# One part of x is loaded by ScalarE's queue instead of SyncE's in a decoder-layer kernel

## What is computed

```python
h = rmsnorm(x, norm_mix_g[l])
proj = jnp.einsum('bsd,de->bse', h, w_in[l])
dq, dk, dv, mq, mk, mv, gate = jnp.split(proj, SPLITS, axis=-1)
...
y = jnp.concatenate([d_out, m_out], axis=-1) * jax.nn.silu(gate)
x = x + jnp.einsum('bse,ed->bsd', y, w_out[l])
h2 = rmsnorm(x, norm_mem_g[l])
mn = rmsnorm(mem, mem_norm_g[l])
q = jnp.einsum('bsd,de->bse', h2, w_q_mem[l]).reshape(B, S, MEM_HEADS, HEAD_DIM)
kv = jnp.einsum('bmd,de->bme', mn, w_kv_mem[l])
...
return rmsnorm(x, final_g)
```

## Time and profile before

| | us |
|---|---|
| median of 3 runs | 571.14 (571.1 to 571.47) |
| the profiled execution, whole run | 571.27 |
| its span, from the first to the last instruction | 569.5 |
| TensorE busy | 560.7 (98% of the span) |
| VectorE busy | 428.2 (75%) |
| ScalarE busy | 408.7 (72%) |
| bytes moved | 123.58 MB, 217 GB/s on the mean |

### The profile page before, as it was taken

One profiled execution on the slowest core, in us unless ns is written; L12 is line 12 of the kernel. 1 busy time (PEld: TensorE's weight loads), 2 busy tenths in 40 slices (PEclk: granted clock), 3 DMA queues, 4 the chain that ended last, 5 costly groups with the idle time before them and its releaser, 6 DMA issues.

```text
span 569.5 us, 8631 instructions
## 1 busy us (share of the span) xinstructions
PE 560.7 (98%) x2648; PEld 467.8 (82%) x2648; DVE 428.2 (75%) x722; ACT 408.7 (72%) x654; POOL 2.1 (0%) x26
## 2 busy tenths in 40 slices
PE   8999999999999999999999999999999999999994
PEld 7888888888888888888888888888888888888884
DVE  5779768688886877866766768667578886878975
ACT  5796866877868778775784784875598796856543
POOL 1000000000000000000000000000000000000000
PEclk9999999999999999999999999999999999999998
DMA  8997769668676776875975976779899986983803
GB/s 264 353 294 236 213 180 217 186 214 231 191 232 193 200 217 187 237 222 156 258 213 157 266 193 202 211 196 290 267 223 280 269 242 194 258 228 110 254 1 147
DMA packets 152292, 123.58 MB, mean 217 GB/s; under 512 B 67865, under 2 KB 134218, under 8 KB 151754
## 3 DMA queue, kind: packets, MB, share of 16 engines
q1 hardware_dynamic: 151946, 122.73, 76.3%
q10 hardware_dynamic: 320, 0.53, 0.3%
HBM read 105.93 MB, written 2.10 MB: 190 GB/s over the span
## 4 chain that ended last, share of the span: by engine, by line
PE 97%; DMA 1%; DVE 1%; ACT 0%; SPq 0%; issue 0%; ACTq 0%
PE ps L643 28%; PE ps L644 28%; PE ps L645 28%; PE ps L725 2%; PE ps L707 1%; PE ps L678 1%; PE ps L682 1%; PE ps L686 1%; PE ps L875 1%; PE ps L880 1%; PE ps L876 1%; DMA xs<-in_x 1%; PE ps L665 1%; PE ps L843 0%; PE ps L710 0%; PE ps L849 0%
## 5 line engine op out<-in xcount | busy, mean ns | idle before, releaser
L1238 DVE TENSOR_TENSOR w_lo<-w_raw,w_hi 128x1024 fp32r<-128x1024 f32 x183 | 222.5, 1222 | 102.9 <-ACT w_hi L905 100.8
L905 ACT ACTIVATE w_hi<-w_raw 128x1024 fp32r<-128x1024 f32 x183 | 192.6, 1057 | 79.4 <-PE ps L645 78.2
L643 PE MATMUL ps<-w_hi,aT 128*128 128x512 f32 x540 | 211.7, 392 | 0.0
L644 PE MATMUL ps<-w_lo,aT 128*128 128x512 f32 x540 | 210.3, 389 | 0.0
L645 PE MATMUL ps<-w_hi,aT 128*128 128x512 f32 x540 | 210.2, 389 | 0.0
L645 PEld LDWEIGHTS ps<-w_hi,aT 128*128 128x128 f32 x540 | 101.4, 188 | 21.3
L643 PEld LDWEIGHTS ps<-w_hi,aT 128*128 128x128 f32 x540 | 101.4, 188 | 20.9
L644 PEld LDWEIGHTS ps<-w_lo,aT 128*128 128x128 f32 x540 | 101.4, 188 | 20.4
L643 PE MATMUL ps<-w_hi,yT_hi 128*128 128x512 f32 x144 | 56.1, 390 | 0.0
L645 PE MATMUL ps<-w_hi,yT_lo 128*128 128x512 f32 x144 | 56.0, 389 | 0.0
L644 PE MATMUL ps<-w_lo,yT_hi 128*128 128x512 f32 x144 | 56.0, 389 | 0.0
(11 more groups left out here) (213 smaller groups left out, 580.9 us busy)
## 6 DMA issues: line engine op xcount, KB each, us to landing
w_raw<-in_w_in SPq DMA_DIRECT2D x251, 256.0 KB, 3.2
w_raw<-in_w_out SPq DMA_DIRECT2D x64, 256.0 KB, 4.1
w_raw<-in_w_kv_mem SPq DMA_DIRECT2D x32, 256.0 KB, 4.2
w_raw<-in_w_q_mem SPq DMA_DIRECT2D x16, 256.0 KB, 3.0
w_raw<-in_w_o_mem SPq DMA_DIRECT2D x16, 256.0 KB, 3.9
mems<-in_mem SPq DMA_DIRECT2D x1, 2048.0 KB, 11.0
xs<-in_x SPq DMA_DIRECT2D x3, 512.0 KB, 5.7
w_raw<-in_w_in SPq DMA_DIRECT2D x10, 128.0 KB, 4.8
```

Source lines behind the costliest of these rows:

```text
L643: pe.matmul(acc, hi[:, k0 + k, tok], w_hi[:, slot, k], start=first and k == 0, stop=False)
L644: pe.matmul(acc, hi[:, k0 + k, tok], w_lo[:, slot, k], start=False, stop=False)
L905: act.activation(w_hi[:, i % SPLITS], raw, ACT.Copy).then_inc(hi_made, 1)
L1238: dve.tensor_tensor(lo, w_raw[:, i % RAW], hi.bitcast(F32), ALU.subtract).then_inc(lo_made, 1)
```

## The change

The second part of x (part 1, columns 256 to 512) leaves SyncE's list: half 1 has no part of x ahead of it there. ScalarE issues the same transfer, with the same semaphore, behind its warm-up activation and ahead of its wait for `gainsT_ready`. Nothing else differs.

```diff
-X_PART_BEFORE = (0, 1, 2, None, 3, None, None, 4)
+X_PART_BEFORE = (0, None, 2, None, 3, None, None, 4)
+X_PART_BY_ACT = 1
...
             act.activation(warm, warm, ACT.Exp).then_inc(warm_ready, 1)
 
 
+            a, b = X_PARTS[X_PART_BY_ACT]
+            act.dma_start(xs[:, :, a:b], x_tiles[:, :, a:b]).then_inc(x_loaded[X_PART_BY_ACT], 16)
             act.wait_ge(gainsT_ready, 1)
```

## The result

The changed kernel takes 571.92 us on the median of 22 executions, against 571.33 for the kernel before on the same chips (22 executions). The ratio is 1.0017 with a 95% interval of 1.0010 to 1.0025: it is slower by about 1 us (the means are 0.93 us apart, the medians 0.59). The forecast was 571.5 and "no change", but the kernel did move, by 0.93 us on the mean where +0.37 was forecast.

A forecast was written before the change was run, and what follows sets the result against it. TensorE was taken to bound the kernel, with transfers able to shift only its start at 7.72 us. A 0.5 us delay of half 0's second plane gave 571.14 + 0.37 = 571.5 us, range 570.8 to 572.2.

The forecast's parts named there:

- What bounds the kernel: TensorE carries 97% of the chain and never waits after 7.72 us; a shift there carries to the end one for one.
- Its issue stays at 2.75: Part 1 of x, moved to ScalarE's queue, would still be issued at 2.75 us, after the warm-up activation.
- rival (c): ScalarE's queue goes on during its table load: x part 1 issued near 1.3 us, earlier transfers late, 571.8 us; chance 0.09.
- The bound of 0.68 us: Most that half 0's transfers could be delayed by part 1 of x: its cost in one queue, 0.68 us.
- H0a: Transfer of half 0's first plane, landing at 5.16 us before, without slack; its delay was bounded by 0.68 us.
- X1: Transfer of part 1 of x (262 KB), the one moved; forecast to land at or before 7.65 us.
- X1 has no more bytes to put in front: Reason given for bounding the delay of H0a by the same 0.68 us.
- Rival (b): Late H0a widens TensorE's gap before row block 0 to 1.0 us, clock stays at half pace: 573.7 us; chance 0.07.
- The gap of today does not: Argument against Rival (b): the existing 0.31 us gap before row block 0 does not keep the clock down.
- the granted clock behind the last matmul: Argument against Rival (b): at the kernel's end it still reads 1.00 in a 1 us stretch without one matmul.
- The sum itself: Row block 1's start: 7.78 + 0.50 - 7.91 = +0.37 us, through a late H0c; chance 0.60.
- H0c: Second slab of half 0's second plane, landing at 6.97 us before; forecast late by 0 to 0.68 us, taken as 0.5.

The follow-up runs named there:

- the 574.0 execution: One profiled execution of the changed kernel, unaltered, taken to catch a slow one: 574.0 us.
- the 572.23 execution: One more profiled execution of the changed kernel, unaltered, with nearly the same landings as the 574.0 execution: 572.23 us.

## Why the prediction was wrong

**What bounds the kernel** was right: in the profiles of the changed kernel only the landings ahead of 8 us count, the shift of row block 2 is carried to the end one for one, and TensorE never waits behind it. But the prediction took the start at 7.72 us to be all that can shift; in the 574.0 execution row block 1 was 2.31 us late (10.22 for 7.91) and row block 2 was 2.75, because the matmuls between them were slower.

**"Its issue stays at 2.75"** is the step that failed first. In the part on what is moved I took the issue to stand behind the activation because its line does, though I had written in rival (c) that it needs nothing of the table load, and gave it 0.09. That the table load starts behind the first issue shows at most that an issue holds up the engine's work written behind it; I took it to hold the other way round too. The profile after has the issue at 1.29, and the run with the issue held at 2.76 has none of the long executions: this timing is what makes them. Of what rival (c) went on to say, one sign did not show: part 0 of x took 2.6 to 2.9 us to land in the five profiles of the changed kernel (3.1 before), so it was not late.

**The bound of 0.68 us** for what H0a can lose failed next. It was X1's cost in one queue at 7 us, where the engines move 356 GB/s. Before 4 us they moved 60 and 261 GB/s in the rows that I had the earlier trace rows. H0a landed at 5.36, 6.1, 6.5, 6.5 and 6.5 us in the five profiles of the changed kernel against 5.16, up to 1.3 us late. The low early rate is not the whole reason, and neither are X1's bytes. Up to 4.0 us the DMA engines had moved 540 KB in the kernel before (135 GB/s on the mean) and 504 KB in the 574.0 execution (126), little less. But when H0a landed, they had moved 857 KB before (166 GB/s to 5.16 us) and 1296 KB there (201 to 6.45): 439 KB more, where X1 has 262. So more of what was issued behind H0a than X1 alone went ahead of its landing, and "X1 has no more bytes to put in front" bounds nothing.

**Rival (b)**, with 0.07, had the mechanism right and the chance wrong. I gave 573.7 for a gap of 1.0 us before row block 0 and a pace that stays at half; measured is 574.0. The terms differ: 0.37 and 2.2 us in my sum, 0.9 for the late half and 1.8 for the pace in the run, so that the totals are near is in part luck. Nor does the gap decide by itself: of the four profiles of the changed kernel with gaps of 1.07 to 1.52 us only one ran at half pace. Two of the arguments against it were bad. "The gap of today does not" says nothing of one three to five times as long. And the granted clock behind the last matmul is a reading of a column that is silent on this: in the 574.0 execution the stretches of half pace read 1.00 as well (columns as in rows 8):

```profile
8.00:9.00 1.00, 1.00 (x4) 0.80 (x3) 0.81 (x2) 0.00 (x0) 0.00 (x0) 1.00 1.05 379
9.00:10.00 1.00, 1.00 (x4) 0.61 (x3) 0.00 (x0) 0.00 (x0) 0.00 (x0) 1.00 1.09 380
```

Four matmuls have a part in each of these microseconds, against seven in the same stretches of the 572.23 execution. I had seen the column contradict the durations of the first transposes and still used it.

**The rivals as separate outcomes.** I set (c) and (b) as two cases with a single time each. In the 574.0 execution they are one chain, early issue, late half 0, gap, slow pace, and long times don't come in each execution: 19 of 44 executions of the changed kernel in all runs lie above 572.5 us. A median hardly shows that (it moves by 0.4 to 1.3 us in the three timed groups), and the mean moves by 0.9 to 1.3 us.

**The sum itself**, +0.37 us, was made for an issue at 2.75 and came near for the kernel that has it: +0.48 on the median, with an interval of the ratio that takes in 1. But its term was another, so that it came near is luck. I had H0c late by 0.5 us and X1 landing at or before 7.65; in the profile H0c was early by 0.3 and X1 late by 0.7 (8.36). The packet-by-packet turns of the Trainium skill ("DMA: Bandwidth & Descriptors", "Queues, rings and completion order") would have H0c land later than in one queue, since X1 takes turns with it. In this one profile it landed earlier (6.7 against 6.97), so I can't say that this trace agrees. In the changed kernel, where H0a and X1 are issued 0.03 to 0.05 us apart on two queues, they landed 0.15 to 0.63 us apart, which fits turns.

**Left open:** why one-queue order with X1 behind H0a has long executions in 3 of 12; what decides, at equal gaps, when the pace rises; and which share of H0a's delay is the second queue and which the earlier bytes, since X1 ahead of H0a in one queue delays it as much (6.4).

## What to carry to other kernels

An issue that was written behind an activation on the same engine was not held by it here (1.29 to 1.30 us in seven profiles, with the table load running to 2.5): if its time matters, make it wait for the activation's semaphore, and look in the first profile where it stands. In the first microseconds of a kernel, a late first operand can cost twice, as a wait and as slower matmuls behind it. Small matmuls up to the first real one, as long as the latest landing and not the usual one, took the long executions away here, but not the loss: the changed kernel with them stayed 0.62 us above before on the mean, so the landing itself comes first. And when a change lies in the start, time it by its single executions, because one profile can show a gain where the mean shows a loss.

## What the hardware showed that was not expected

TensorE's pace doubles at a time that differs between executions of one kernel with the same gaps: before 7.26 us in one and near 11 us in another (572.23 and 574.0 us). In a third execution (573.96, with four turns behind the transposes) it stayed at half until after 10.29 us, though the engine had worked without a gap since 4.83. The two paces are told by the distance of equal matmuls, 0.43 and 0.23 us for 512 columns, which fit the levels of 1.2 and 2.4 GHz. The granted clock reads 1.00 in all three and doesn't tell. The mean granted clock of whole executions does not follow it either: 0.996 in both.

The landing of one and the same first transfer of 256 KB, issued at 1.26 us, differs by 1.1 us between executions (4.1 to 5.2 us on its way) once a second transfer of 256 KB is issued beside it.
